# Norms by token quarters and packed mixer input tiles in a two-layer hybrid attention encoder

## The reference

```python
def rmsnorm(x, g):
    y = xf * lax.rsqrt(jnp.mean(xf * xf, axis=-1, keepdims=True) + EPS)
    return (y * g.astype(jnp.float32)).astype(x.dtype)

def ffn_half(x, pre_g, w_up, w_down, post_g):
    h = rmsnorm(x, pre_g)
    gate, up = jnp.split(h @ w_up, 2, axis=-1)
    y = (jax.nn.silu(gate) * up) @ w_down
    return x + 0.5 * rmsnorm(y, post_g)

    # mixer
    u = rmsnorm(x, P['mix_pre_gain'][l])
    (q_lat, kv_lat, k_r, q_b, k_b, v_b, q_c, k_c, v_c, q_i, k_i, w_i,
     g_a, g_b, g_c) = jnp.split(u @ P['w_in'][l], IN_OFFSETS, axis=-1)
```

## Time and profile before

| | |
|---|---|
| median of 3 runs | 3212.32 µs (3211.82 to 3215.07) |
| the profiled execution | 3217.1 µs, its span 3215.3 µs |
| busy: TensorE / its weight loads | 3045.0 µs / 2817.9 µs (95% / 88%) |
| busy: VectorE / ScalarE / GpSimd | 1521.5 / 1009.8 / 1069.8 µs |
| mean granted TensorE clock | 0.98 of full speed |

### The profile page before, as it was taken

One profiled execution on the slowest core, in us unless ns is written; L12 is line 12 of the kernel. 1 busy time (PEld: TensorE's weight loads), 2 busy tenths in 40 slices (PEclk: granted clock), 3 DMA queues, 4 the chain that ended last, 5 costly groups with the idle time before them and its releaser, 6 DMA issues. The chain is left out here.

```text
span 3215.3 us, 53586 instructions
## 1 busy us (share of the span) xinstructions
PE 3045.0 (95%) x22902; PEld 2817.9 (88%) x22902; DVE 1521.5 (47%) x1645; ACT 1009.8 (31%) x1615; POOL 1069.8 (33%) x499
## 2 busy tenths in 40 slices
PE   8999979999999989999899999799999999899997
PEld 7999977966878989999899999779567789899997
DVE  4554241763345446553265542328623554555523
ACT  3222223353445232222232222333634452322221
POOL 3344323312232424434334434223022324243432
PEclk9999989999999999999999999899999999999998
DMA  6221232111111222222212222322121113122221
GB/s 179 79 91 68 90 111 96 60 55 57 50 57 57 89 94 81 89 83 73 106 66 83 87 73 98 101 80 76 40 67 50 63 54 116 66 92 78 79 82 64
DMA packets 43099, 255.44 MB, mean 79 GB/s; under 512 B 6048, under 2 KB 6144, under 8 KB 26048
## 3 DMA queue, kind: packets, MB, share of 16 engines
q1 hardware_dynamic: 37008, 235.64, 21.0%
q0 software_dynamic: 5840, 17.50, 2.0%
q10 hardware_dynamic: 96, 0.08, 0.0%
HBM read 237.34 MB, written 15.85 MB: 79 GB/s over the span
## 5 line engine op out<-in xcount | busy, mean ns | idle before, releaser
L419 POOL TENSOR_TENSOR ring_r<-ring,piece_h 128x1024 fp32r<-128x1024 f32 (+1 forms) x240 | 630.2, 2627 | 1025.8 <-ACT piece_h L1108 1025.8
L419 POOL TENSOR_TENSOR ring_r<-ring,piece_m 128x1024 fp32r<-128x1024 f32 (+1 forms) x172 | 369.1, 2151 | 866.4 <-ACT piece_m L1108 866.1
L1108 ACT ACTIVATE piece_h<-ring 128x1024 fp32r<-128x1024 f32 (+1 forms) x240 | 274.9, 1147 | 1151.2 <-PE PS L620 1142.5
L615 PE MATMUL PS<-uT_r,piece_h 128*128 128x272 f32 x2688 | 555.9, 288 | 6.1 <-DVE sq L1512 6.1
L615 PE MATMUL PS<-u_l,piece_h 128*128 128x272 f32 x2688 | 556.3, 288 | 0.0
L620 PE MATMUL PS<-uT_r,ring_r 128*128 128x272 f32 x3328 | 451.1, 288 | 0.0
L620 PEld LDWEIGHTS PS<-uT_r,ring_r 128*128 128x128 f32 x3328 | 430.0, 188 | 0.0
L615 PEld LDWEIGHTS PS<-uT_r,piece_h 128*128 128x128 f32 x2688 | 420.9, 188 | 7.0 <-ACT piece_h L1108 7.0
L615 PEld LDWEIGHTS PS<-u_l,piece_h 128*128 128x128 f32 x2688 | 421.1, 188 | 0.0
L615 PE MATMUL PS<-act_l,piece_h 128*128 128x272 f32 x1408 | 292.4, 290 | 0.0
L615 PE MATMUL PS<-act_h,piece_h 128*128 128x272 f32 x1408 | 291.7, 288 | 0.0
(11 more groups left out here) (235 smaller groups left out, 4637.0 us busy)
## 6 DMA issues: line engine op xcount, KB each, us to landing
ring<-in_w_up SPq DMA_DIRECT2D x88, 1024.0 KB, 4.8
ring<-in_w_dn SPq DMA_DIRECT2D x64, 704.0 KB, 4.1
ring<-in_w_mg SPq DMA_DIRECT2D x48, 768.0 KB, 4.4
ring<-in_w_in SPq DMA_DIRECT2D x24, 1024.0 KB, 4.8
ring<-in_w_out SPq DMA_DIRECT2D x8, 1024.0 KB, 4.9
x_spill<-xT SPq DMA_DIRECT2D x2, 2176.0 KB, 8.7
xT<-x_spill SPq DMA_DIRECT2D x2, 2176.0 KB, 8.5
ring<-in_w_vb SPq DMA_DIRECT2D x4, 1024.0 KB, 4.8
```

The lines of the kernel that those rows point to most:

```text
L419: nc.gpsimd.tensor_tensor(ring_r[:, ch[0] % NSLOT, at:at + n], w, hi, ALU.subtract).then_inc(S["w_low"], 1)
L615: mm(PS[:, 2 * u + b, 0:HALF], w, x[k][:, HALF * b:HALF * b + HALF], start=first and k == 0 and n == 0, stop=False)
L1108: A(buf[:, hs, 0:n], ring[:, ch % NSLOT, at:at + n], ACT.Copy).then_inc(S["w_high"], 1)
```

## The change

The change has three parts. **Norms by token quarters:** for six of the eight norms of a layer (all but those of the two latents) the sum is taken by four matmuls with 32 columns of ones and 136 tokens each (QUARTER). Quarter j of the tokens comes out on partitions 32j to 32j+31 of bank 4, so root and reciprocal work on 128x136 (`root_q`). A new function `spread` copies the result back to all partitions with four matmuls of one row of ones into banks 6 and 7 (unit 3), two, a wait for their end, then two. VectorE's scaling reads unit 3 in PSUM in place of `rstd` in SBUF; in a feed-forward block ScalarE copies it to `rstd`, and `spread` stands between the last matmuls of the first pair. **Packed tiles:** kI and kC become one tile, kk, whose halves ScalarE copies out four times; the tile vw also holds the 32 features of kr; kr and krs are made from it by one small fp32 product each with a 32x128 matrix of ones and zeros. The mixer has 27 pieces in place of 30, and the values of branch B come in four chunks of 1024 columns. **One move:** VectorE selects the keys of block 4 behind the rotation of qr and qs, just ahead of attention, in place of ahead of branch B.

```diff
+QUARTER = TOK // 4
+SPREAD = {n: i for i, n in enumerate(("pre_a", "post_a", "mix", "mix_post", "pre_b", "post_b"))}
...
-    t = ["kI"] + [f"qI{i}" for i in range(4)] + ["kC", "vw", "v0", "v1"]
+    t = ["qI0", "qI1", "kk", "qI2", "qI3", "vw", "v0", "v1"]
...
+            def sum_quarters(x, first, last):
+
+                for j in range(4):
+                    ins = mm(PS[32 * j:32 * j + 32, 4, 0:QUARTER], ones[:, 0:32], x[:, QUARTER * j:QUARTER * j + QUARTER],
+                             start=first, stop=last, skip_group_check=True)
+                return ins
+
+            def spread(l, norm):
+
+                pe.wait_ge(S["inv"], l * N_NORM + NORMS[norm][0] + 1)
+                n = l * len(SPREAD) + SPREAD[norm]
+                for half in range(2):
+                    for bank in (6, 7):
+                        j = 2 * (bank - 6) + half
+                        ins = mm(PS[:, bank, QUARTER * half:QUARTER * half + QUARTER], ones[32 * j:32 * j + 1, :],
+                                 root_q[32 * j:32 * j + 1, :], start=half == 0, stop=True, skip_group_check=True)
+                        if half == 0:
+                            ins.then_inc(S["spread_first"], 1)
+                    if half == 0:
+                        pe.wait_ge(S["spread_first"], 2 * n + 2)
+                        alone(pe)
+                ins.then_inc(S["spread"], 1)
...
+                    if k == KD + LAG - 2 and spread_at_end:
+                        spread(l, spread_at_end)
...
-                for i in range(15, 30):
-                    name = TILES[9 + i - 11]
-                    split_tile(name, u_h, u_lo, IN_PIECES[i][0], IN_PIECES[i][1])
+                for i, name in enumerate(("kr", "krs")):
+                    tile(name, [(cst[64:96, 6 + i, :], vw_f[64:96, 0:TOK])])
+                for name in LATE_TILES[4:]:
+                    split_tile(name, u_h, u_lo, *IN_PIECES[PIECE_OF[name]][:2])
...
+                if norm in SPREAD:
+                    A(root_q, PS[:, 4, 0:QUARTER], ACT.Sqrt, scale=1.0 / (K * P), bias=eps_c[:]).then_inc(S["root"], 1)
+                    return
...
+                act.wait_ge(S["spread"], l * len(SPREAD) + SPREAD[pre] + 1)
+                A(rstd[:].rearrange("p (a b) -> p a b", a=2), unit(3)[:, :, 0:HALF], ACT.Copy).then_inc(S["rstd_in"], 1)
...
-                    V.scalar_tensor_tensor(out=y[:, k, :], in0=y[:, k, :], scalar=g_of(l, c0 + k), in1=rstd[:],
-                                           op0=ALU.mult, op1=ALU.mult).then_inc(S["yscaled"], 1)
+                    V.scalar_tensor_tensor(out=halves(y[:, k, :]), in0=halves(y[:, k, :]), scalar=g_of(l, c0 + k),
+                                           in1=unit(3)[:, :, 0:HALF], op0=ALU.mult, op1=ALU.mult).then_inc(S["yscaled"], 1)
...
-                select(l, 4, 3)
                 dve.wait_ge(S["rows_ki"], 16 * (l * 2 + 2))
                 branch_b(l)
...
+                select(l, 4, 4)
                 attend(l, 0)
                 attend(l, 1)
```

More of the change, by code:

```diff
@@ L70 @@
 PC_FFN = 2 * KF + 2 * KD
-PC_MIX = 30 + 48 + 8
+N_IN = 27
+PC_MIX = N_IN + 48 + 8
 PC_A, PC_M, PC_B = 0, PC_FFN, PC_FFN + PC_MIX
@@ L105, in mixer_tiles @@
     t += [f"uq{i}" for i in range(4)] + ["qr0", "qs0", "qr1", "qs1"]
-    t += [f"kA{i}" for i in range(4)] + [f"vA{i}" for i in range(4)]
+    t += [f"kA{i}" for i in range(4)] + [f"vA{i}" for i in range(4)] + ["pad"]
     return t + [f"wo{n}" for n in range(KD)]
@@ L118 @@
 TILE = {name: i for i, name in enumerate(TILES)}
+V_CHUNKS = 4
+LATE_TILES = TILES[8:12] + TILES[14:27]
 MIX_CHUNKS = ([("w_in", i, 2048, TILES[2 * i + 1]) for i in range(3)]
-              + [("w_vw", 0, 1024, "vw"), ("w_vb", 0, 2048, "v1"), ("w_vb", 1, 2048, "v1")]
-              + [("w_in", 3 + i, 2048 if i < 9 else 1024, TILES[min(10 + 2 * i, 27)]) for i in range(10)]
+              + [("w_vb", i, 1024, f"V{i}" if i + 1 < V_CHUNKS else "v1") for i in range(V_CHUNKS)]
+              + [("w_in", 3 + i, 2048 if i < 8 else 1024, LATE_TILES[min(2 * i + 1, 16)]) for i in range(9)]
               + [("w_uq", 0, 1536, "uq3"), ("w_uq", 1, 1536, "qs1"), ("w_ukn", 0, 1024, "kA3"), ("w_ukv", 0, 1024, "vA3")]
@@ L598, in sum_partitions @@
                 pe.wait_ge(S["sq_used"], l * N_SQ + q0 + K + 1)
-                for b in range(2):
-                    mm(PS[:, 4 + b, 0:HALF], ones, rstd[:, HALF * b:HALF * b + HALF], start=True, stop=False)
+                sum_quarters(rstd, True, False)
                 pe.wait_ge(S["sq_ready"], l * N_SQ + q0 + K)
-                for b in range(2):
-                    ins = mm(PS[:, 4 + b, 0:HALF], ones, sq[:, (K - 1) % 2, HALF * b:HALF * b + HALF], start=False, stop=True)
-                ins.then_inc(S["sq_used"], 1)
+                sum_quarters(sq[:, (K - 1) % 2, :], False, True).then_inc(S["sq_used"], 1)
+                spread(l, norm)
             def split_product(l, u, piece, hs, w_l, x_h, x_l, first=True, last=True, buf=piece_m):
@@ L688, in mixer @@
                     square_sum(l, "mix", k)
+                spread(l, "mix")
                 ch = CH_M
@@ L706, in mixer @@
                            piece_m)
-                for i in range(2, 7):
+                for i in range(2, 6):
                     split_tile(TILES[i], u_h, u_lo, IN_PIECES[i][0], IN_PIECES[i][1])
@@ L765, in mixer @@
                     at = (i % 4) * KQ * P
-                    tile(TILES[28 + i], [(w[:, at + k * P:at + k * P + P], ql[:, k, :]) for k in range(KQ)])
+                    tile(TILES[27 + i], [(w[:, at + k * P:at + k * P + P], ql[:, k, :]) for k in range(KQ)])
                     if i == 0:
@@ L1433, in invert, with rstd_of @@
                 dve.wait_ge(S["inv"], l * N_NORM + j + 1)
+            def rstd_of(l, norm):
+                invert(l, norm, root_q)
+                dve.wait_ge(S["spread"], l * len(SPREAD) + SPREAD[norm] + 1)
             def pre_norm(l, norm, v, u_f, u_lo):
-                invert(l, norm)
+                rstd_of(l, norm)
                 c0 = NORMS[norm][1]
@@ L1444, in pre_norm @@
                 for k in range(KD):
-                    V.scalar_tensor_tensor(out=u_f[:, k, 0:TOK], in0=xT[:, k, :], scalar=g_of(l, c0 + k), in1=rstd[:],
-                                           op0=ALU.mult, op1=ALU.mult).then_inc(S["u_norm"], 1)
+                    V.scalar_tensor_tensor(out=halves(u_f[:, k, 0:TOK]), in0=halves(xT[:, k, :]), scalar=g_of(l, c0 + k),
+                                           in1=unit(3)[:, :, 0:HALF], op0=ALU.mult, op1=ALU.mult).then_inc(S["u_norm"], 1)
                     if k:
```

115 lines of the change are left out of this document (67 added, 48 removed).

## The result

The changed kernel takes 3165.60 µs (median of 4 runs, 3163.76 to 3168.24), the kernel before 3213.49 (4 runs). The ratio is 0.9852, its 95% interval 0.9836 to 0.9868. The profiled execution took 3163.76 µs with a span of 3161.2. Forecast were 3165 µs, and 3169.7 for a profiled execution.

The account below looks back on a forecast made before the run. TensorE bounds the kernel, busy 3045.0 of 3215.3 µs. Packed tiles 30.7, output norms 12.7, mixer's norm 2.0 and first pairs 2.0 sum to 47.4 µs: 3169.7 profiled, 3165 median, range 3152 to 3178 (trusted 0.8).

Parts of the forecast that it names:

- Packed tile kk: In the mixer, kk in place of kI and kC saves one tile, 6.04 µs a layer, ScalarE's copies hidden.
- kr and krs: Between qC3 and ql0, two small products and one wait: 12.08 µs saved, 2.7 cost, net 9.3 a layer.
- Selection 4: Just ahead of attention it costs nothing; in its old place VectorE would be about 2 µs late at branch B.
- One norm: Quartered sum, root and reciprocal gain 0.1, 0.4 and 2.6 µs, the spread costs 2.25: net 0.9 µs.
- Rival B: The spread is cheap, 1.1 µs in all; seven places gain 1.1 each: 3157 µs; chance 0.17.
- Output norms: At six norms, scalings from PSUM escape GpSimd's wait, the first addition takes it: 2.0 µs at five, 12.7 in all.
- Mixer's norm: The norm ahead of the mixer, twice: 0.9 µs and 0.06 from the first scaling, 2.0 in all.
- rival E: Behind norms TensorE stays at half clock longer; 20 µs longer at each of seven restarts gives 3235 µs; chance 0.04.
- First pairs: Four feed-forward first pairs: quarter sums 0.65 µs each, spread 1.9; gains 0.6 at first, 0.5 at others: 2.0 in all.
- A: In first pairs, narrow sums pay at both ends, 0.17 µs a passage, 11 µs: about 3175 µs; chance 0.18.
- C: At its new place the selection comes late, stretched by GpSimd's subtractions, say 8 µs a layer: 3181 µs; chance 0.04.
- D: The saved tiles turn into waits for ScalarE's copies or VectorE's chain, packing brings nothing: 3196 µs; chance 0.02.

## Why the prediction was right, and where not

- **Packed tile kk**: 6.04 µs a layer, as priced from the earlier trace rows. Right; the copies of kk cost TensorE nothing.
- **kr and krs**: 7.6 net and not 9.3. The cost was put at 2.7 µs from qC3 to ql0; it is 3.18 in the changed kernel, and the tile behind it runs at half clock at first, 1.2 µs more. The waits were priced right and the clock was missing: where no half clock comes (the first layer of the kernel with full first pairs, among others) the way is 2.84 and the stage gains 9.14. With ScalarE's order turned the way is 2.02, so of those 2.84 some 0.8 were its weight copy.
- **Selection 4**: "With selection 4 in its old place VectorE would be late by about 2 µs" was wrong. VectorE is free 21.9 µs ahead of its first use, 16.0 are needed, and in the old place it waits 7.23 µs. The step measured VectorE's chain from the last indexer step as if it were all work. It held a wait of 3.63 µs for TensorE's tiles (for the root of the key latents), which went as those tiles came sooner, and some 2 µs of stretched operations. It cost the sum nothing, since the move was priced at nothing too.
- **One norm**: root 0.37 for 0.30, reciprocal 1.00 for 0.93; last sum to root 0.51 where 1.19 stood, so 0.7 gained and not 0.1; the spread 1.30 from its start to the scaling and not 2.25. The term of the spread is the one most in error. The step took L603's way of 1.19 for each group. But L603 was four records of full width; a group of the spread steps 0.69, and 0.61 leads to VectorE. Rival B had the better price for it, 1.1: the last norm gained 2.45 for 1.2.
- **Output norms**: mechanism right, shown from three sides (scaling from SBUF, GpSimd moved, longer spread): scalings with an operand in PSUM are not stretched beside GpSimd (781 ns at most), and the first addition takes the wait. Gain 2.47 each, 14.8 with the last norm, for 12.7. The 1.8 for faster scalings were wrong: they take 775 ns, as before (778 in the earlier trace rows), not 0.72. In their place GpSimd's end came 1.0 sooner against the sums and not 0.5.
- **Mixer's norm**: 1.44 each up to the first pair, 1.21 and 1.48 with it, for 1.0. The spread was cheap but at half clock: each of its two groups steps 1.01 µs (444.36 to 445.37) and not 0.69. Here rival E is seen in small: half clock lasts from 429.1 to 453.0, where before there was full clock from 440.9 to 451.1. It costs the spread 0.6 and little more, since in the sums TensorE waits for ScalarE's squares and at the first pair for VectorE's remainder.
- **First pairs**: 5.1 by the traces, 2.9 by the ratio of the experiment, for 2.0. A sum costs 0.36 with passages of 0.09 and 0.10, so 0.55 and not 0.65, the spread 1.12 and not 1.9; the wait at the second tile is 0.98 as predicted. At the three pairs behind a norm the gain is 0.5 to 0.7 each, near the 0.5 predicted, where half clock is short; the rest of the 5.1 is what the full-width form loses at long half clock, and the pair at the start, whose length varies between profiles. The forecast had neither.
- **The sum**: the priced places gained 12.1 + 15.25 + 14.8 + 2.7 + 5.1 = 49.9 for 47.4, as an excess at the norms that a shortfall at kr and krs hid in part. The profiled execution came out 5.9 µs under the forecast for it: 2.5 by the priced places, 5.8 at the values, less 1.5 lost elsewhere and 0.8 outside the span. That the median was hit to 0.6 µs is luck. Before, the profiled execution lay 3.6 µs over the median of the four runs, and after, it lies 1.8 under; the prediction took 4.8 over for both. That error of 6.6 cancels the 5.9.
- **Rivals**: A is refuted by the passages of 0.09 and 0.10 µs, where it needed 0.17 each, and by the kernel with full first pairs, which is not faster. B named the term that was too dear. Of the seven times 1.1 µs that it gave the cheap spread, the last norm had 1.25, the mixer's norms 0.44 each, and the first pairs nothing that can be told from the clock, so the time is not its 3157. C: the selection ended 9.23 µs before the first maximum, not late. D: TensorE reached branch B after VectorE, and the packed tiles paid. E: half clock lasted longer at two norms, at a cost of about 1 µs in all.

What stays open: what decides whether a wait of 1 to 3 µs is followed by half clock. Profiles of one kernel agreed and those of kernels with edits elsewhere did not, but executions of one kernel differ as well; no run set the timing on purpose or profiled one kernel often enough.

## What to carry to other kernels

When VectorE and GpSimd work at the same time, look at which VectorE operations have both operands in SBUF and when GpSimd starts; moving one operand to PSUM or GpSimd's start by a few µs was worth 1.1 to 1.8 µs at each of the five output norms with GpSimd beside them. When you ask how long an engine's chain will last once its place moves, take the waits out of it first: they go along with what they wait for. And when a gain turns up in a stage that the change does not touch, read the granted clock there before explaining it, since it can be gone in the next kernel or the next execution (6.0 µs in one profile here). Compare the times of all executions too: the profiled one can be the fastest.
